# First layer norm and modulation, worked by feature tile: another order of loads, sums, factors and modulation at the start of a two-layer encoder kernel

## What is computed

```python
D_MODEL = 1024; SEQ = 512; DEPTH = 2
x = layer_norm(x, ln_in_g, ln_in_b)
c_act = jax.nn.silu(c)
for l in range(DEPTH):
    mod = c_act @ w_ada[l] + b_ada[l]
    sh1, sc1, g1, sh2, sc2, g2 = jnp.split(mod, 6, axis=-1)
    h = x * (1.0 + sc1) + sh1
    z = h @ w_in[l]
    # four mixers on slices of z (gating, attention, S5, HGRN2)
    x = layer_norm(DN_ALPHA * x + (1.0 + g1) * (ym @ w_out[l]), ln1_g[l], ln1_b[l])
    # second modulation, gated MLP with a short convolution, third norm
```

## Time and profile before

| | |
|---|---|
| median of 3 runs | 1385.88 us (1385.84 to 1388.8) |
| profiled execution | 1380.86 us, span 1379.1 us |
| busy: TensorE matmul | 1333.1 us (97%) |
| busy: TensorE weight load | 996.0 us (72%) |
| busy: VectorE | 879.6 us (64%) |
| busy: ScalarE | 512.8 us (37%) |
| busy: GpSimd | 217.5 us (16%) |
| mean granted TensorE clock | 0.983 |
| chain that ended last | PE 82%, DVE 11%, issue 2%, DMA 2%, POOL 2%, ACT 1% |

### The profile page before, as it was taken

The page is one execution under the profiler, slowest core; times in us unless marked ns, Lnnn a source line. Parts: engine busy times, 40 slices in busy tenths (PEclk is TensorE's granted clock), DMA queues, the critical chain, the costliest instruction groups (busy, mean ns, idle before and its releaser), DMA issues.

```text
span 1379.1 us, 17249 instructions
## 1 busy us (share of the span) xinstructions
PE 1333.1 (97%) x6866; PEld 996.0 (72%) x6866; DVE 879.6 (64%) x1523; ACT 512.8 (37%) x770; POOL 217.5 (16%) x193
## 2 busy tenths in 40 slices
PE   6898999999999999999999999999999999999997
PEld 3445776786888888888855577777678888888886
DVE  5986878766877777767663456675765555563335
ACT  2524224335533334433233422343363333343223
POOL 0640200635000000000047010053420000000003
PEclk9999999999999999999999999999999999999998
DMA  9456733021666666755225341102223333323321
GB/s 384 166 122 168 173 119 111 17 93 61 216 192 186 185 187 188 255 190 173 77 92 95 76 79 35 44 19 77 62 92 93 96 102 92 92 92 92 96 89 62
DMA packets 64801, 166.79 MB, mean 121 GB/s; under 512 B 14288, under 2 KB 26960, under 8 KB 64208
## 3 DMA queue, kind: packets, MB, share of 16 engines
q1 hardware_dynamic: 64720, 165.68, 40.0%
HBM read 160.04 MB, written 5.62 MB: 120 GB/s over the span
## 4 chain that ended last, share of the span: by engine, by line
PE 82%; DVE 11%; issue 2%; DMA 2%; POOL 2%; ACT 1%; SPq 0%; ACTq 0%; POOLq 0%; DVEq 0%
PE bank L496 19%; PE bank L498 19%; PE bank L497 18%; PE bank L587 7%; PE bank L581 3%; PE bank L612 2%; PE bank L511 2%; PE bank L516 1%; PE bank L740 1%; PE bank L777 1%; PE bank L505 1%; PE bank L1020 1%; DVE ada L1220 1%; PE bank L560 1%; DMA cf<-in_consts 1%
## 5 line engine op out<-in xcount | busy, mean ns | idle before, releaser
L496 PE MATMUL bank<-ym_r,scr_r 128*128 128x512 f32 x688 | 274.0, 398 | 4.7 <-DVE hm_r L1785 2.5
L498 PE MATMUL bank<-hm_r,scr_r 128*128 128x512 f32 x688 | 273.1, 397 | 0.0
L497 PE MATMUL bank<-ym_r,ring_r 128*128 128x512 f32 x688 | 270.4, 393 | 0.0
L1228 DVE TENSOR_TENSOR ring_r<-ring,scr_r 128x1024 fp32r<-128x1024 f32 x134 | 165.6, 1236 | 89.6 <-ACT scr_r L1940 89.4
L1940 ACT ACTIVATE scr_r<-ring 128x1024 fp32r<-128x1024 f32 x146 | 153.2, 1051 | 133.1 <-DMA ring<-in_w_down 110.6
L496 PE MATMUL bank<-scr_r 128*128 128x512 f32 x480 | 192.9, 402 | 2.1 <-DVE ym_r L1721 1.9
L497 PE MATMUL bank<-scr_r,ring_r 128*128 128x512 f32 x480 | 187.6, 391 | 0.0
L587 PE MATMUL bank<-hm,ring 128*128 128x512 f32 x336 | 158.0, 610 | 0.0
L496 PEld LDWEIGHTS bank<-ym_r,scr_r 128*128 128x128 f32 x688 | 129.3, 188 | 38.3 <-issue 6.1
L498 PEld LDWEIGHTS bank<-hm_r,scr_r 128*128 128x128 f32 x688 | 129.3, 188 | 32.3
L497 PEld LDWEIGHTS bank<-ym_r,ring_r 128*128 128x128 f32 x688 | 128.7, 187 | 32.3
(11 more groups left out here) (370 smaller groups left out, 1783.3 us busy)
## 6 DMA issues: line engine op xcount, KB each, us to landing
ring<-in_w_up SPq DMA_DIRECT2D x88, 512.0 KB, 3.7
ada<-in_w_ada SPq DMA_DIRECT2D x80, 512.0 KB, 3.7
ring<-in_w_down SPq DMA_DIRECT2D x44, 512.0 KB, 3.6
ring<-in_w_in SPq DMA_DIRECT2D x33, 512.0 KB, 4.9
scr<-in_w_ada SPq DMA_DIRECT2D x16, 512.0 KB, 14.4
ring<-in_w_out SPq DMA_DIRECT2D x16, 512.0 KB, 3.7
pa<-in_par_a SPq DMA_DIRECT2D x2, 2144.5 KB, 13.1
xa<-in_x SPq DMA_DIRECT2D x1, 2048.0 KB, 8.2
```

Of the source, the lines that this page charges most:

```text
L496: first = mm(dst, w_hi, x_hi, start=start, stop=False)
L497: mm(dst, w_lo, x_hi, start=False, stop=False)
L498: return first, mm(dst, w_hi, x_lo, start=False, stop=stop)
L1228: V.tensor_tensor(ring_r[:, slot(l, n), :], ring[:, slot(l, n), :], high[:, slot(l, n), :].bitcast(F32), ALU.subtract)\
```

## The change

It touches only the first norm and its modulation.

- **Loads.** c comes as one row of one partition, first; then the constants, then x in four transfers of two tiles. The tiles of `w_ada` come in pairs (scale tile k, shift tile k), and the first two projection chunks after the fourth pair.
- **c.** TensorE spreads it over the partitions (two matmuls with one row of ones), and ScalarE applies silu from the two banks.
- **Sums.** The identity matmuls and the two copies are gone. `norm_sums` runs on each tile of x and each tile of squares, and all accumulate in the same columns of bank 7.
- **Order on VectorE.** Four pairs, then the norm's small operations, then tiles 0 and 1 normalised in one operation of each kind (`first_apply`), a pair, tiles 2 and 3, a pair, tiles 4 and 5, two pairs, tile 6, tile 7.
- **Gains.** GpSimd makes them in four groups (`first_gains`), before the tiles that need them (`first_stream`).
- **Semaphores.** `x_in` becomes four, a few others are merged, and counts are adapted.

```diff
-            sp.dma_start(xa[:, :, :], x).then_inc(S["x_in"], 16)
-            sp.dma_start(silu_c[:, :], c_row).then_inc(S["c_then_out"], 16)
+            sp.dma_start(silu_c[0:1, :], c_row[0:1, :]).then_inc(S["c_then_out"], 16)
             sp.dma_start(cf[:, 0:CF_FIRST], consts[:, 0:CF_FIRST]).then_inc(S["const_in"], 16)
-            for i in range(MOD_PRE):
-                sp.dma_start(early[i], w_ada[0, i]).then_inc(early_in[i // 2], 16)
+            for i in range(KD // 2):
+                sp.dma_start(xa[:, 2 * i:2 * i + 2, :], x[:, 2 * i:2 * i + 2, :]).then_inc(x_in[i], 16)
...
+            for k in range(KD):
+                for i in (KD + k, k):
+                    sp.dma_start(early[i], w_ada[0, i]).then_inc(early_in[k], 16)
+                if k == 3:
+                    load(0, 0)
+                    load(0, 1)
...
-            pe.wait_ge(S["x_in"], 16)
-            for k in range(KD):
-                last = mm(banks[4][:, :], ident, xa[:, k, :], start=(k == 0), stop=(k == KD - 1))
-            last.then_inc(S["ln_accx"], 1)
-            for k in range(KD):
-                pe.wait_ge(S["ln_sq"], k + 1)
-                last = mm(banks[5][:, :], ident, hm[:, k, :], start=(k == 0), stop=(k == KD - 1))
-            last.then_inc(S["ln_accq"], 1)
-            norm_pause(1)
+            pe.wait_ge(S["c_then_out"], 16)
+            for i in range(2):
+                last = mm(banks[4 + i][:, :], ones[0:1, :], silu_c[0:1, i * T:(i + 1) * T], start=True, stop=True)
+            last.then_inc(S["c_spread"], 1)
+            for i in range(KD // 2):
+                pe.wait_ge(x_in[i], 16)
+                for k in (2 * i, 2 * i + 1):
+                    norm_sums(xa[:, k, :], 64, k == 0, k == KD - 1)
+                for k in (2 * i, 2 * i + 1):
+                    pe.wait_ge(S["ln_sq"], k + 1)
+                    last = norm_sums(hm[:, k, :], 68, False, k == KD - 1)
+            last.then_inc(S["ln_stat"], 1)
+            keep_awake(1)
+            norm_spread(1)
+            keep_awake(2)
...
-            for i in range(MOD_PRE):
-                modulation(i, mods[:, i:i + 1])
-                if i == STATS_AFTER:
-                    norm_var(1)
-                if i == STATS_AFTER + 1:
-                    norm_rstd(1)
-            v.wait_ge(S["ada_used"], MOD_PRE)
-            modulated(0, 0)
-            norm_apply(1)
-            v.wait_ge(S["const_rest"], 16)
+
+            def first_modulation(k):
+                for i in (KD + k, k):
+                    modulation(i, mods[:, i:i + 1])
+
+            def first_apply(k, n):
+
+                def wide(bank):
+                    return bank[:, :].rearrange("p (o t) -> p o t", o=1).to_broadcast([P, n, T])
+
+                v.wait_ge(S["ln_bcast"], 1)
+                ch.link(V.tensor_tensor(xa[:, k:k + n, :], xa[:, k:k + n, :], wide(banks[0]), ALU.mult))
+                v.wait_ge(S["ln_bcast"], 2)
+                V.tensor_tensor(xa[:, k:k + n, :], xa[:, k:k + n, :], wide(banks[1]), ALU.subtract)\
+                    .then_inc(S["ln_normed"], n)
+
+            for k in range(4):
+                first_modulation(k)
+            norm_var(1)
+            norm_rstd(1)
+            first_apply(0, 2)
+            first_modulation(4)
+            first_apply(2, 2)
+            first_modulation(5)
+            first_apply(4, 2)
+            first_modulation(6)
+            first_modulation(7)
+            first_apply(6, 1)
+            first_apply(7, 1)
+            v.wait_ge(S["const_in"], 32)
...
+            a.wait_ge(S["c_spread"], 1)
+            A(silu_c[:, 0:T], banks[4][:, :], ACT.Silu)
+            A(silu_c[:, T:D], banks[5][:, :], ACT.Silu).then_inc(S["silu_then_raw"], 1)
             for k in range(KD):
+                a.wait_ge(x_in[k // 2], 16)
                 norm_square(None, k, k)
...
+            def first_gains(k0, k1):
+
+                at = slice(k0, k1)
+                sh, sc = mod[:, k0:k1], mod[:, KD + k0:KD + k1]
+                g.wait_ge(S["ada_used"], 2 * k1)
+                ch.post(G.tensor_tensor(sc, mods[:, KD + k0:KD + k1], c_f("b_ada")[:, KD + k0:KD + k1], ALU.add))
+                ch.post(G.tensor_tensor(sh, mods[:, k0:k1], c_f("b_ada")[:, k0:k1], ALU.add))
+                ch.settle()
+                ch.link(G.tensor_scalar(sc, sc, 1.0, 1.0 / ALPHA, ALU.add, ALU.mult))
+                ch.post(G.tensor_tensor(gh[:, 0, 0, at], ga[:, 0, at], sc, ALU.mult))
+                ch.post(G.tensor_tensor(gh[:, 0, 1, at], ga[:, 1, at], sc, ALU.mult))
+                ch.settle()
+                return G.tensor_tensor(gh[:, 0, 1, at], gh[:, 0, 1, at], sh, ALU.add)
...
+            ch.link(first_gains(0, 4))
+            first_stream(0, 2)
+            ch.link(first_gains(4, 5))
+            first_stream(2, 4)
+            ch.link(first_gains(5, 6))
+            first_stream(4, 6)
+            first_gains(6, 8).then_inc(S["h_par"], 1)
+            g.wait_ge(S["h_par"], 1)
+            first_stream(6, 8)
```

More of the change, by code:

```diff
@@ L83 @@
 MOD_LAG = 2
-STATS_AFTER = 11
 MOD_AT = {p + 2: (2 * (p - 5), 2 * (p - 4)) for p in range(5, NPROJ)}
@@ L302, in sems @@
             return {n: ctx.enter_context(nc.semaphore(n)) for n in names}
+        x_in = [ctx.enter_context(nc.semaphore(f"x_in{i}")) for i in range(KD // 2)]
         ada_in = [ctx.enter_context(nc.semaphore(f"ada_in{i}")) for i in range(ARING)]
@@ L433, in s5_traffic @@
                     sp.wait_ge(S["s5_k"], l + 1)
-                    sp.wait_ge(S["s5_zero"], 16)
+                    sp.wait_ge(S["c_then_out"], 32)
                     for e in range(SC):
@@ L442, in s5_traffic @@
                         sp.dma_start(toe[16 * e:16 * e + 16, :, :], k_d[:, :, 16 * e:16 * e + P]).then_inc(S["s5_toe"], 16)
+            for k in range(KD):
[4 more added lines that the diff above has]
+                    load(0, 1)
             sp.wait_ge(S["s5_mag"], 1)
-            sp.dma_start(k_d[:, :, 0:(SC - 1) * 16], zero[0:16, :].rearrange("p (g x) -> p g x", g=NG)).then_inc(S["s5_zero"], 16)
+            sp.wait_ge(S["c_then_out"], 16)
+            sp.dma_start(k_d[:, :, 0:(SC - 1) * 16], zero[0:16, :].rearrange("p (g x) -> p g x", g=NG)).then_inc(S["c_then_out"], 16)
             for l in range(L):
-                if l == 0:
-                    load(l, 0)
-                    load(l, 1)
                 if l == 0:
@@ L453, in _ @@
                     sp.dma_start(pa[:, :], par_a[l]).then_inc(S["para_in"], 16)
-                    sp.dma_start(cf[:, CF_FIRST:CF_N], consts[:, CF_FIRST:CF_N]).then_inc(S["const_rest"], 16)
+                    sp.dma_start(cf[:, CF_FIRST:CF_N], consts[:, CF_FIRST:CF_N]).then_inc(S["const_in"], 16)
                 for n in range(NCHUNK):
@@ L469, in _ @@
                 sp.dma_start(out[:, k, :], xa[:, k, :]).then_inc(S["c_then_out"], 16)
-            sp.wait_ge(S["c_then_out"], 16 * (KD + 1))
+            sp.wait_ge(S["c_then_out"], 16 * (KD + 2))
         @block.tensor
@@ L520, in norm_stats @@
             def norm_stats(n, late=None):
-                pe.wait_ge(S["ln_sumx"], n)
+                pe.wait_ge(S["ln_sumx"], n - 1)
                 norm_sums(acc[:, 0, :], 64, True, late is None)
-                pe.wait_ge(S["ln_sumq"], n)
+                pe.wait_ge(S["ln_sumq"], n - 1)
                 last = norm_sums(acc[:, 1, :], 68, False, late is None)
@@ L1212, in modulation @@
                 w = early[f]
-                v.wait_ge(early_in[f // 2], 32)
+                v.wait_ge(early_in[f % KD], 32)
                 V.scalar_tensor_tensor(w, w, 1.0, silu_c[:, :], ALU.mult, ALU.mult, accum_out=dst).then_inc(S["ada_used"], 1)
@@ L1926, in _ @@
             A(small[:, 92:93], c_f("half_pi"), ACT.Sqrt)
[L1927 to L1930, removed]
             norm(1)
@@ L1965, in _ @@
                 if l == 0:
-                    a.wait_ge(S["const_rest"], 16)
+                    a.wait_ge(S["const_in"], 32)
                     A(c_f("rope_s")[QK:P, :], c_f("rope_s")[NOPE:QK, :], ACT.Identity).then_inc(S["q_tab"], 1)
@@ L2271, in modulate, with first_stream @@
                     low(KD - 1)
+            def first_gains(k0, k1):
[10 more added lines that the diff above has]
+                return G.tensor_tensor(gh[:, 0, 1, at], gh[:, 0, 1, at], sh, ALU.add)
+            def first_stream(k0, k1):
+                for k in range(k0, k1):
+                    g.wait_ge(S["ln_normed"], k + 1)
+                    G.tensor_scalar(hm[:, k, :], xa[:, k, :], gh[:, 0, 0, k:k + 1], gh[:, 0, 1, k:k + 1],
+                                    ALU.mult, ALU.add).then_inc(S["h_ready"], 1)
+            g.wait_ge(S["const_in"], 16)
+            g.wait_ge(S["ln_par"], 1)
+            ch.link(first_gains(0, 4))
[7 more added lines that the diff above has]
+            first_stream(6, 8)
             for l in range(L):
-                modulate(2 * l + 1, 0)
-                g.wait_ge(S["const_rest"], 16)
+                if l:
+                    modulate(2 * l + 1, 0)
```

(3 more changed lines are left out.)

9 lines of the change are left out of this document (3 added, 6 removed).

## The result

| | before | changed |
|---|---|---|
| median, runs | 1386.85 us, 4 | 1396.58 us, 4 |
| ratio, 95% interval | | 1.0063, 1.0039 to 1.0086 |
| profiled execution, its span | 1380.86, 1379.1 us | 1396.21, 1394.4 us |
| mean granted TensorE clock | 0.983 | 0.980 |
| first S5 operation of VectorE that waits for ScalarE | 50.5 us | 64.11 us |

One of the four runs took 2206.52 us at a mean granted clock of 0.56; the ratio leaves it out, and without it the median is 1396.21. The change makes the kernel slower, by 0.6 to 1.0%.

The account below looks back on a forecast made before the run. VectorE, not TensorE, was taken to carry the time until about 115 us. Late statistics put its last subtraction at +13.4 us and GpSimd's last tile at +13.2, taking 1385.88 us to 1399.1; range 1393.5 to 1403.5.

Parts of the forecast that it names:

- Start: Kernel start: constants land at about 5.0 us, four low-clock records take 3.4 us, c is spread at 8.9.
- First pair: First modulation tiles' transfer: comes 1.24 us earlier, at 12.15 us, with 508 KB less ahead of it.
- Statistics: First norm's sums on TensorE: 128 single-column records at 0.213 us, 27.3 us, from 8.9 to 36.2.
- a clock that is high throughout: Rival for the sums: high clock, sums end at 23.8 us, last h 0.6 us sooner, median 1385.3; chance 0.12.
- for one stretch: Rival for the sums: high clock for 3.4 us, sums end 3.4 us sooner, median 1395.7; chance 0.18.
- The break-even point: First norm: statistics at 24.5 us change nothing; any later, each us is one of loss.
- From the statistics on: VectorE after the sums: first multiply 39.8 us, first subtraction begins 41.5, last subtraction ends 59.5 against 46.13, +13.4 us.
- GpSimd: Gains and last h tiles: six small operations at 0.33 us, two tiles of 0.77, last at 60.4 us, +13.2.
- the rival of dear ones: Rival on GpSimd: small operations at 0.85 us, last six 5.1 us, last h at 63.5, median 1402.2; chance 0.09.
- TensorE: First two projection chunks: start about 43.5 us, end at 63, 8 us later; less than VectorE's 13, so slack unused.
- Sum: Whole kernel: +13.2 us, profiled execution 1380.86 to 1394.1, median 1399.1 us, 1.0% slower; chance 0.58.

Follow-up runs that it names:

- e7: e6 with x in one transfer and the statistics' operations behind one more pair; 1383.84 us, ratio 0.9971.
- e6: e1 with projection chunks behind all w_ada tiles, statistics' operations after pairs five and six, normalisation after all modulation, gains in one group; 1383.76 us, ratio 0.998.
- e1: The changed kernel with the sums made as before: 512-column identity matmuls, two copies, 16 single-column matmuls; 1386.49 us, ratio 1.0001.
- e5: The changed kernel with four more 512-column matmuls, output unread, between the spread of c and the first sum; 1405.19 us, one run.
- e0: The kernel before, run once more with no edit; 1391.77 us, one run.
- e4: The changed kernel, run once more with no edit; 1400.42 us, ratio 1.0100 against the kernel before.
- e2: The changed kernel with all eight modulation pairs ahead of the statistics on VectorE and GpSimd's gains in one group; 1390.27 us, ratio 1.0034.

## Why the prediction was right

The forecast was 1399.1 us, slower by 1.0%; measured were 1396.58 and, a second time, 1400.42, both within the range. Its steps:

**Start.** The constants were put at 5.0 us and land at 4.0; c is spread at 8.3 (8.9), since the four records take 3.7 us (3.4). The sums therefore begin 0.6 us before their time.

**First pair: the one step that failed.** "The first pair comes 1.24 us earlier (508 KB less ahead of it)", at 12.15. It came at 13.70, 0.3 later than before. The saved bytes were there, but x in four pieces moved at 305 instead of 398 GB/s, and e7, with x in one piece, has the pair 0.9 us earlier (12.78); the other 0.6 us stay open. It cost the sum nothing, because VectorE waited 12.12 us behind these tiles; it is felt where the statistics are early, as in e6.

**Statistics: the term that decides.** 128 x 0.213 = 27.3 us was forecast; the rows below are from TensorE's timeline of the changed kernel, around the first and the last of the eight groups of 16 records:

```profile
4.61 3.77 PE L562 MATMUL bank<-silu_c,cf 1*128 1x512 f32 x4
8.31 3.57 PE L518 MATMUL bank<-cf,xa 128*128 128x1 f32 x16
...
32.23 3.55 PE L518 MATMUL bank<-cf,hm 128*128 128x1 f32 x16
35.64 2.05 PE L537 MATMUL bank<-cf 128*128 128x512 f32 x2
37.49 3.62 PE L513 MATMUL bank<-cf,st 128*128 128x128 f32 x16
```

From 8.31 to 35.64 are 27.3 us. The prediction's reading of the earlier trace rows was right, although not all 33 records of the earlier trace rows are "such records": the end of a series of 512 columns is among them. The Trainium skill (TensorE: Matmul & The Clock Gate, section LDWEIGHTS (loading the stationary operand)) has a formula that gives 107 ns for a load of 128 columns, which is an estimate worked out from it. That fits the sixteen records of e1 at 2.4 GHz, 0.11 us each, not the 128 here. The rivals of a clock that is high throughout, or for one stretch, did not come; e5 made their condition by force, and even then only about 21 records were fast. In e5 the sums had the high clock for 2.3 us (from 13.77 us to about 16) and took 25.0 us instead of 27.3: each us of high clock gives one back, which is how the prediction priced its stretch of 3.4 us.

**The break-even point.** Statistics at 24.5 us were said to be neutral. e1 has them at 26.48, which is 2.0 us of loss by that rule, and shows 2.7. It holds to 0.7 us.

**From the statistics on.** The first multiply was put at 39.8 and starts at 39.44, the first subtraction at 41.5 (41.25), the last subtraction ends at 59.16 (59.5).

**GpSimd.** The small operations cost 0.19 or 0.20 us each instead of 0.33, the last group of six 1.3 instead of 2: the rival of dear ones is out. Only two of the 24 were dear, 1.25 and 1.16 us, and both ran beside a modulation tile (below). But the tiles of h were priced at 0.77 each, and the six that ran beside the modulation took 1.2 to 2.3 each on the mean of their pairs (below). The last is done at 60.79 us, where 60.4 was forecast: two errors that nearly cancel.

**TensorE.** It was to start the first two chunks at 43.5 and end at 63, and did at 45.45 and 64.1; it is late because the first tiles of h are. Nothing waits for it, as said: its wait for VectorE at 115 us grew.

**Sum.** +13.2 us was forecast, +13.6 measured at the first S5 operation. The way from that to a median carries a scatter of several microseconds, as e0 and e4 show, which is why the two measurements, +9.7 and +14.8 us, lie on both sides of it. Between the two profiled executions nothing but the 13.6 us of the start and 1.7 us at a lower clock was added, 15.3 in all. That the median came within 3 us of the forecast is in part luck; that the start came within 0.4 is not, but for GpSimd's end, where two errors met.

## What to carry to other kernels

Price a block of single-column fp32 matmuls at the low clock: doing the sums directly on every tile needs no copies and fewer columns, yet took 27 us where adding the tiles up first with wide matmuls took 18. And before splitting a phase to start its consumer sooner, see whether the result it waits for is early enough: work moved behind a late result is no longer its cover (e2: 9.3 us). Where a piece-wise load is meant to bring a start forward, compare the rate in GB/s of the pieces with that of the whole.

## What the runs showed of the hardware

**GpSimd stands still beside some VectorE operations.** GpSimd's timeline in the changed kernel:

```profile
42.65 3.41 POOL L2316 TENSOR_SCALAR hm<-xa,gh 128x512 f32<-128x512 f32 x2 [17.42 <-DVE xa L1267]
...
47.14 1.25 POOL L2310 TENSOR_TENSOR gh<-gh,mod 128x1 f32<-128x1 f32 x1
48.49 2.39 POOL L2316 TENSOR_SCALAR hm<-xa,gh 128x512 f32<-128x512 f32 x2
...
58.83 0.20 POOL L2310 TENSOR_TENSOR gh<-gh,mod 128x2 f32<-128x2 f32 x1
```

the modulation tile of VectorE that the second row fell in with:

```profile
47.12 1.22 DVE L1222 SCALAR_TENSOR_TENSOR scr<-scr,silu_c 128x1024 f32<-128x1024 f32 x1
```

and in e2, where the modulation is over before GpSimd begins:

```profile
43.20 1.52 POOL L2315 TENSOR_SCALAR hm<-xa,gh 128x512 f32<-128x512 f32 x2 [4.97 <-DVE xa L1267]
```

Two tiles take 1.52 us beside VectorE's normalisation, and 3.41, 2.39 or 4.52 (the pair at 53.22 us) where its modulation is in the way; each of these three ends 1.3 to 1.5 us after the last modulation tile beside it. The operation on 128x1 at 47.14 us took 1.25 us where its like took 0.19, and ended with VectorE's tile. The modulation reads two operands of 128x1024 from SBUF, the normalisation one from SBUF and one from a bank. The Trainium skill, SBUF — State Buffer, section Who interferes with whom, has this rule: a VectorE instruction with two SBUF inputs contends with a GpSimd instruction that reads SBUF, one with at most one SBUF input, outside what the page calls 2-port perf modes (no run here tests those), doesn't. The rows agree, for these two kinds of VectorE operation.

**The granted clock does not show a clock that has not yet risen.** The sums of the changed kernel, by stretch, in the columns used above:

```profile
8.00:36.00 28.00, 28.00 (x130) 27.69 (x130) 9.70 (x18) 6.71 (x12) 1.11 (x6) 1.00 1.03 413
```

It reads 1.00, with the records 0.213 us apart; in e5, with the same spacing, it reads 0.50. The mean of 0.980 for the changed kernel therefore counts 28 slow microseconds as full speed. At a kernel's start, the spacing of equal records tells the level and the column does not.

**Equal kernels, unequal clocks.** Starts repeat within half a microsecond; what differs from run to run (1380.86 and 1391.77 us, one kernel) comes later, together with the mean granted clock (0.983 and 0.975), in steps such as the 1.7 us at 115 us (e0). What decides how often the clock is taken back there was not tried.
